# A hybrid decoder block on eight cores: row tiles transposed earlier, five weight places, a spread bias table and residual rows in pieces

## The chip, the cores and the metric

The kernel is one program on the 8 NeuronCores of one Trainium2 chip, four on each die. Cores 2b and 2b+1 share batch row b: each computes 8 of its 16 blocks of 128 tokens and projects keys and values for all 16. Nothing passes between cores. The metric is the device time of the slowest core in microseconds (us).

## The reference, cut to what matters

```python
h = _rmsnorm(x, norm1_g)
q, k, v, q_i, k_i, w_i, u_b, v_b, g_a, g_b = _split_cols(h @ w_in)    # 10320 columns
q, k, k_i = rmsnorm(q), rmsnorm(k), rmsnorm(k_i)                      # per head of 128; k_i: 64
score = sum_h w_i[t, h] * relu(q_i[t, h] . k_i[s]); sel = top_k(score, 256)    # causal
out_a = softmax(q . k[sel] * scale + rel_bias[t5_bucket(t - s)]) @ v[sel]      # 8 heads of 128
out_b = gelu(u_b) * (tril(w_spatial) @ rmsnorm(gelu(v_b)) + b_spatial)
merged = sigmoid(g_a) * (out_a @ w_proj_a) + sigmoid(g_b) * (out_b @ w_proj_b)
x = x + merged @ w_out
x = x + (silu(h2 @ w_ffn_gate) * (h2 @ w_ffn_up)) @ w_ffn_down        # h2 = rmsnorm(x)
```

## The kernel before, in words

Engines get their instructions from Python lists. `Prog` adds the waits: each `Buf` remembers its last writer and its readers, and an engine waits for those semaphores in its own order. A later instruction never overtakes a waiting one, on any engine or DMA queue. A normalized chunk of four tiles has one `Buf` (`B_h[hx]`), so a projection that reads one tile waits for the last tile written into that chunk.

`Dense` is a list of small steps with costs. `unit` adds one output tile as steps of four matmuls, in one of three PSUM banks; `norm_post` sends a Square to ScalarE (ACT) at once and the rest (a matmul with ones at L425, Ln, Exp, and the scaling on VectorE, DVE) one step later. `Stream` holds the weights in order, 256 columns a block: two DMAs of 512 KB as bf16 from the POOL queue, cast on the way. A place is loaded again when its block was last used. Before, the ring has three places.

**The first list, D0**, has these stages. In the v stage, row tiles 0 to 7 are loaded by SP (`x_load`, three buffers), normalized (`x_norm`: Square, Ln, Exp on ACT, one scaling on DVE), transposed on PE (L405, 16 transposes into banks 5 and 6), copied out by ACT and DVE, and projected by v blocks 0 to 3. `prep` puts the norm of tile t+1 ahead of the transposition of tile t. In the k stage, 16 units (4 blocks) alternate with the bias table: `table_item` makes one of 16 tables with two matmuls in one bank (L534), two Exps into one of four buffers `e1`, and a store of 192 KB to `fscr` by SP; tables (0, h) and (1, h) use the same buffer. `xt` transposes tiles 8 to 15 during k and q. Then come two units of the indexer's key (ki), 16 of q, 16 of the indexer's query (qi) and 8 small ones of its weights (wi, 16 columns).

**Attention** (441 to 1141 us in the profile) works through 8 query blocks. A second list, DD, is pulled into it by shares of estimated time: two ki units, the other half of k and v, and the gates g_a and g_b, whose tanh goes to `gscr`.

**The third list, D3**, has the v_b and u_b projections, the spatial gating (`sgu_z`), the projections by w_pa and w_pb in blocks of 8 matmuls per bank, w_out, and the feed-forward part. `gl_load` fetches the gates again (8 DMAs of 256 KB for each c2), and `x1_load` fetches the residual rows (8 tiles of 1 MB). The latter stands 40 steps, five blocks, ahead of the end of w_pa/w_pb for six tiles, and at the end for two.

Of the kernel before, what the change touches and what calls it, by code (L numbers as in the profile page):

```python
# [8 lines left out]
BF16 = mybir.dt.bfloat16  # L9
# [168 lines left out]
def build(ncores=8):  # L178
# [31 lines left out]
    with ExitStack() as es:  # L210
# [66 lines left out]
        RING = [R(3 + 8 * i, 8 * KB, BF16, "p (c n) -> p c n", c=16) for i in range(3)]  # L277
        B_ring = [Buf('ring%d' % i) for i in range(3)]
# [21 lines left out]
        class Stream:  # L300


            def __init__(self):
                self.specs = []
                self.left = {}
                self.got = {}
                self.next = 0
# [4 lines left out]

            def load(self, i):
                slot, b = RING[i % 3], B_ring[i % 3]
# [9 lines left out]
            def pump(self):  # L324
                while self.next < len(self.specs) and (self.next < 3 or self.left.get(self.next - 3) == 0):
                    self.load(self.next)
                    self.next += 1
# [61 lines left out]
        def norm_tile(xb_, xn_, Bxb, Bxn, scol, Bs, Bg):  # L389
            sc = st[:, scol:scol + 3]  # L390
            act(xn_, xb_, AF.Square, (Bxb,), (Bxn, Bs), accum_out=sc[:, 0:1])
            act(sc[:, 1:2], sc[:, 0:1], AF.Ln, (Bs,), (Bs,), scale=1.0 / D, bias=EPS)
            act(sc[:, 2:3], sc[:, 1:2], AF.Exp, (Bs,), (Bs,), scale=-0.5)
            dve('stt', (Bxb, Bs, Bg), (Bxn,), out=xn_, in0=xb_, scalar=sc[:, 2:3], in1=GB, op0=ALU.mult, op1=ALU.mult)
# [20 lines left out]
        norm_banks = {'b': [3, 4], 'n': 0}  # L415
# [27 lines left out]
        def x_load(i):  # L443
            dma_sp(XB[i % 3], x_perm[i * 128:(i + 1) * 128, :], (), (B_xb[i % 3],))
# [14 lines left out]
        x_load(2)  # L459
# [25 lines left out]
        def ki_block():  # L485
            sp = []
            for j in range(2):
                for dup in range(2):
                    sp.append((w_in[j * 1024:(j + 1) * 1024, 4096:4160], 8 * j, 64 * dup))
            return WS.block(sp)  # L490
# [39 lines left out]
        def table_item(q, h):  # L530
            i4 = (q * 8 + h) % 4
            pi = 7
            for u0, u1 in ((0, 512), (512, 768)):
                P.op('pe', lambda e, u0=u0, u1=u1: e.matmul(psb[pi][:, 0:u1 - u0], Lh[:, h, :], oh3[:, q, u0:u1],  # L534
                                                            start=True, stop=True), (B_lh, B_oh), (PS[pi],))
                act(e1[i4][:, u0:u1], psb[pi][:, 0:u1 - u0], AF.Exp, (PS[pi],), (B_e1[i4],))
            base = (q * 8 + h) * 128 * 768
            dma_sp(Fscr[base:base + 128 * 768].rearrange("(r u) -> r u", u=768), e1[i4], (B_e1[i4],), (B_F[q * 8 + h],))
# [48 lines left out]
        def xt():  # L587
# [16 lines left out]
        for hx in (HO0, HT0):  # L604
            ki_unit(D0, kib, hx)
# [7 lines left out]
        B_qTn = [Buf(), Buf()]  # L613
        for b in range(4):
            for cc in range(2):
                for n in range(2):
                    q_unit(qb[b], b, cc, n)
            D0.add(0.5, xt)

# [5 lines left out]
        def wi_unit(tt):  # L625
            n = tt // 4

            def cons(pi):
                dve('copy', (PS[pi],), (B_wt,), out=wtok[:, tt, :], in_=psb[pi][:, 0:16])
            tm_unit(D0, wib, lambda c: hX[n][:, c, (tt % 4) * 128:(tt % 4 + 1) * 128], B_h[n], 16, cons)  # L630
# [4 lines left out]
        for tt in range(8):  # L635
            wi_unit(tt)
# [3 lines left out]
        kib2 = ki_block()  # L640
# [14 lines left out]
        for hx in (HO1, HT1):  # L655
            ki_unit(DD, kib2, hx)
        DD.mark('ki')
# [314 lines left out]
        for k in range(1, 9):  # L972
            if k == 4:
# [447 lines left out]
```

How the kernel before makes its waits and increments, by code:

```python
            def run(name, e):  # L1301
                for waits, fn, inc in P.q[name]:
                    for k, v in waits:
                        e.wait_ge(sems[k], v)
                    if fn is None:
                        continue
                    ins = fn(e)
                    ins.then_inc(sems[inc[0]], inc[1])
```

## Time and profile before

| | |
|---|---|
| three runs | 2462.30, 2698.13, 2724.69 us; median 2698.13 |
| profiled execution | 2464.36 us, span 2462.8 us (core 3; all cores 2431.7 to 2462.8) |
| busy PE, DVE, ACT, POOL | 87%, 33%, 23%, 10% of the span |
| chain that ended last | PE 69%, DVE 13%, DMA 7%, issue 6%, ACT 4% |
| DMA | 222.43 MB moved, mean 90 GB/s |

One execution is shown, on its slowest core. "L262 <- DVE arena L246" reads: the instruction of line 262 waited for a semaphore that the one of line 246 raised. PE is TensorE's matmul. "Busy" at the granted clock 0.5 means 1.2 GHz, at 1.0 it means 2.4 GHz; a mean between them is a mix of the two.

### The profile page before, as it was taken

Reading aid. Unit: us, or ns where it says so; the run is one execution under the profiler, and the core shown is the slowest. Engines: PE = TensorE matmul, PEld = TensorE weight load, DVE = VectorE, ACT = ScalarE, POOL = GpSimd, SP = SyncE. Lnnn points to the kernel's source line nnn. Section 1 sums busy time; section 2 is a strip of 40 time slices with the busy share of each in tenths; the row PEclk is TensorE's granted clock in tenths of the full one; section 3 lists DMA queues with packets and bytes.
Section 4 is the critical chain, followed back from the end, with each engine's and each line's share of the span. In section 5 each row is a group of like instructions: output and inputs, shape, how many; then the busy total and the mean of one; then the engine's idle time right before and its main releaser. Section 6 shows DMA issues by size and latency. Waiting matters only on the chain.

```text
span 2462.8 us, 36680 instructions; the slowest of 8 cores (2431.7 to 2462.8 us)
## 1 busy us (share of the span) xinstructions
PE 2154.8 (87%) x13626; PEld 1247.6 (51%) x13626; DVE 818.3 (33%) x1589; ACT 562.8 (23%) x945; POOL 240.1 (10%) x280
## 2 busy tenths in 40 slices
PE   3656599777898798989989698999999999999999
PEld 2532244323653434347644386444448864444688
DVE  1101131566776867673155324101111110111111
ACT  2314362334344343444300003100000000000000
POOL 0010011000000000000101110111111111111010
PEclk8878799888999999999999899999999999999999
DMA  8274475422333535357649963656546565555485
GB/s 189 69 98 80 76 119 55 65 35 47 48 52 78 112 69 103 65 108 164 78 71 235 220 85 52 79 74 77 77 62 80 77 86 75 77 78 71 63 146 116
DMA packets 319566, 222.43 MB, mean 90 GB/s; under 512 B 25376, under 2 KB 293920, under 8 KB 316064
## 3 DMA queue, kind: packets, MB, share of 16 engines
q0 software_dynamic: 281152, 137.94, 45.1%
q1 hardware_dynamic: 38240, 82.15, 10.1%
q8 instruction: 112, 1.84, 0.3%
q14 instruction: 62, 0.51, 0.1%
HBM read 329.66 MB, written 29.88 MB: 146 GB/s over the span
## 4 chain that ended last, share of the span: by engine, by line
PE 69%; DVE 13%; DMA 7%; issue 6%; ACT 4%; SPq 1%; DVEq 0%; POOL 0%; ACTq 0%; POOLq 0%
PE ps L262 49%; PE ps L1256 12%; DVE arena L244 8%; ACT arena L239 4%; PE ps L740 3%; DVE arena L243 3%; DMA arena<-w_pb 2%; DMA arena<-w_in 2%; PE ps L752 2%; DVE arena L245 2%; DMA fscr<-arena 1%; DMA arena<-w_out 1%; DMA arena<-c_oh 1%; SPq L253 1%; PE ps L405 1%
## 5 line engine op out<-in xcount | busy, mean ns | idle before, releaser
L262 PE MATMUL ps<-arena 128*128 128x512 bf16 (+2 forms) x8384 | 1618.8, 350 | 101.4 <-DVE arena L246 31.0
L262 PEld LDWEIGHTS ps<-arena 128*128 128x128 bf16 x8384 | 816.3, 100 | 796.6 <-issue 142.2
L239 ACT ACTIVATE arena<-ps 128x512 f32<-128x512 f32 (+4 forms) x459 | 264.9, 580 | 1244.0 <-PE ps L262 1066.8
L1256 PE MATMUL ps<-arena 128*128 128x256 bf16 x2816 | 307.7, 273 | 3.0 <-DVE arena L243 3.0
L1256 PEld LDWEIGHTS ps<-arena 128*128 128x128 bf16 x2816 | 275.4, 98 | 35.7 <-issue 3.9
L243 DVE TENSOR_TENSOR arena<-ps,arena 128x512 bf16<-128x512 f32 (+2 forms) x128 | 84.2, 658 | 585.4 <-PE ps L262 540.4
L239 ACT ACTIVATE arena<-ps,arena 128x512 bf16<-128x512 f32 (+1 forms) x312 | 199.7, 647 | 194.5 <-PE ps L752 86.4
L256 POOL DMA_DIRECT2D arena<-w_in x106 | 92.8, 883 | 1117.5 <-PE ps L262 464.0
L245 DVE SCALAR_TENSOR_TENSOR arena<-arena 128x1 f32<-128x1 f32 (+2 forms) x256 | 107.9, 424 | 273.6 <-ACT arena L239 248.4
L244 DVE TENSOR_SCALAR_CACHE_REDUCE arena<-arena 128x512 bf16<-128x512 f32 (+6 forms) x112 | 173.2, 1546 | 14.4 <-DVE arena L245 0.5
L239 ACT ACTIVATE arena<-arena 128x2048 bf16<-128x2048 f32 (+3 forms) x135 | 97.4, 721 | 278.9 <-DVE arena L245 257.6
L243 DVE TENSOR_TENSOR arena<-arena 128x512 bf16<-128x512 bf16 (+9 forms) x297 | 136.3, 469 | 47.4 <-ACT arena L239 16.6
L244 DVE TENSOR_SCALAR arena<-ps,arena 128x512 bf16<-128x512 f32 (+1 forms) x152 | 107.0, 708 | 117.1 <-PE ps L752 105.4
L243 DVE TENSOR_TENSOR arena<-arena,ps 128x256 f32<-128x256 f32 x128 | 53.9, 421 | 255.8 <-PE ps L1256 250.5
L245 DVE SCALAR_TENSOR_TENSOR arena<-ps,arena 128x256 f32<-128x256 f32 (+1 forms) x116 | 66.1, 569 | 198.2 <-ACT arena L239 128.7
L740 PE MATMUL ps<-arena 128*128 128x512 bf16 (+1 forms) x304 | 89.2, 370 | 20.0 <-ACT arena L239 11.3
L887 PE MATMUL ps<-arena 128*128 128x129 bf16 x576 | 59.4, 221 | 50.7 <-DVE arena L243 24.5
L887 PEld LDWEIGHTS ps<-arena 128*128 128x128 bf16 x576 | 37.6, 98 | 66.7 <-issue 65.1
L256 POOL DMA_DIRECT2D arena<-w_down x48 | 41.1, 859 | 301.7 <-PE ps L1256 227.0
L256 POOL DMA_DIRECT2D arena<-w_up x44 | 38.4, 878 | 303.1 <-PE ps L262 290.9
L534 PE MATMUL ps<-arena 128*128 128x512 bf16 (+1 forms) x32 | 11.7, 365 | 61.5 <-ACT arena L239 49.9
L245 DVE SCALAR_TENSOR_TENSOR arena<-arena,ps 128x512 f32<-128x512 f32 x64 | 43.9, 687 | 57.6 <-PE ps L262 33.3
(39 smaller groups left out, 486.4 us busy)
## 6 DMA issues: line engine op xcount, KB each, us to landing
arena<-w_in POOLq DMA_DIRECT2D x96, 512.0 KB, 7.9
arena<-x_perm SPq DMA_DIRECT2D x24, 1024.0 KB, 9.6
arena<-w_gate POOLq DMA_DIRECT2D x44, 512.0 KB, 7.3
arena<-w_up POOLq DMA_DIRECT2D x44, 512.0 KB, 7.1
gscr<-arena SPq DMA_DIRECT2D x64, 256.0 KB, 2.4
arena<-gscr SPq DMA_DIRECT2D x64, 256.0 KB, 9.4
arena<-w_down POOLq DMA_DIRECT2D x32, 512.0 KB, 7.5
arena<-w_out POOLq DMA_DIRECT2D x16, 512.0 KB, 9.7
```

The lines of the kernel that those rows point to most:

```text
L239: return P.op('act', lambda e: e.activation(out=out, in_=in_, func=func, **kw), reads, writes)
L243: 'tt': lambda e: e.tensor_tensor(**kw),
L244: 'ts': lambda e: e.tensor_scalar(**kw),
L245: 'stt': lambda e: e.scalar_tensor_tensor(**kw),
L253: return P.dma('sp', lambda e: e.dma_start(out=out, in_=in_), reads, writes, append)
L256: return P.dma('pool', lambda e: e.dma_start(out=out, in_=in_), reads, writes, append)
L262: ins = e.matmul(out, pairs[i][0], pairs[i][1], start=(i == 0), stop=(i == n - 1))
L405: ins = e.transpose(pv[:, c * 128:(c + 1) * 128], xn_[:, cc * 128:(cc + 1) * 128], ident)
L740: P.op('pe', lambda e, h=h, rt=rt: e.matmul(psb[G[4]][:, 0:wc], Dg[:, h, :], rt[:, 0:wc], start=(h == 0), stop=(h == 15)), (B_dg, B_rt[(2 ...
L752: P.op('pe', lambda e, a=a, pi=pi: e.matmul(psb[pi][:, 0:wc], qsrc[64 * a:64 * a + 64, p, q0:q0 + 128], kiT2[64 * a:64 * a + 64, c0:c0 + w ...
L887: ins = e.matmul(psb[po][:, hh * 130:hh * 130 + 129], PT[pti][:, (j - g0) * 128:(j - g0 + 1) * 128], V[:, j, h, 0:129], start=(j == 0), st ...
L1256: ins = e.matmul(psb[tt][:, 0:256], aT[:, f0 + c, tt * 128:(tt + 1) * 128], slot[:, c, 0:256], start=(f0 + c == 0), stop=(f0 + c == 21))
```

## The change

In the v stage, tile 1 is transposed ahead of the first projection, and later tiles one to two projections ahead of where they stood; the copies out of PSUM now stand ahead of the next tile's norm on ACT. The ring has five places up to the end of the q blocks (two lie where qi is written later), three after that. Three loads of row tiles (2, 4 and 6) wait until weight blocks 0, 1 and 2 have landed. The table's inputs load at the start; each table is two parts, in banks 4 and 7, one part after every second step of the k stage. All four ki units and the wi units stand between q and qi and use one block of 80 columns, doubled by a DVE copy. The gates' first two loads stand after six v_b units. The residual rows are 32 loads of 256 KB, in four column pieces.

```diff
@@ ring and its places
-        RING = [R(3 + 8 * i, 8 * KB, BF16, "p (c n) -> p c n", c=16) for i in range(3)]
+        RING = [R(o, 8 * KB, BF16, "p (c n) -> p c n", c=16) for o in (3, 11, 19, 111.5, 119.5)]
+            def place(self, i):
+                return i % 5 if i < self.wide else (i - self.wide) % 3
...
-        norm_banks = {'b': [3, 4], 'n': 0}
+        norm_banks = {'b': [3], 'n': 0}
...
@@ v stage
+        GATE = {2: 0, 4: 1, 6: 2}
...
             x_norm(i)
             if i + 3 < 16:
-                x_load(i + 3)
+                x_load(i + 3, (WS.use(GATE[i + 3])[1],) if i + 3 in GATE else ())
 
         WS.pump()
+        x_load(2, (WS.use(GATE[2])[1],))
         xstep(0)
+        xstep(1)
+        table_loads()
+        x_tr(0)
...
-        order = [(0, 0), (1, 0), (2, 0), (0, 1), (1, 1), (2, 1), (3, 0), (3, 1), (4, 0), (4, 1),
-                 (0, 2), (1, 2), (2, 2), (3, 2), (4, 2), (5, 0), (5, 1), (5, 2), (6, 0), (6, 1), (6, 2),
-                 (7, 0), (7, 1), (7, 2)]
...
-                def prep(t=t):
-                    if t + 1 < 8:
-                        xstep(t + 1)
-                    x_tr(t)
-                D0.add(0.5, prep)
+        order = [(0, 0), (1, 0), (2, 0), (3, 0), (0, 1), (1, 1), (2, 1), (3, 1), (4, 0), (4, 1), (5, 0), (5, 1),
+                 (0, 2), (1, 2), (2, 2), (3, 2), (4, 2), (5, 2), (6, 0), (6, 1), (6, 2), (7, 0), (7, 1), (7, 2)]
+        before = {0: 1, 1: 2, 2: 3, 6: 4, 8: 5, 14: 6, 18: 7, 21: 8}
+
+        def x_next(t):
+            x_tr(t)
+            if t + 1 < 16:
+                xstep(t + 1)
+        for n_, (t, b) in enumerate(order):
+            if n_ in before:
+                D0.add(0.5, lambda t=before[n_]: (x_tr(t) if t < 8 else None, xstep(t + 1) if t < 8 else None))
...
@@ k stage
-                D0.add(0.5, lambda b=b, cc=cc: (table_item(0, 2 * b + cc), table_item(1, 2 * b + cc)))
-                if cc == 1:
-                    D0.add(0.5, xt)
+        parts = [(q, h, p) for h in range(8) for q in range(2) for p in range(2)]
+        mixed = []
+        for j, it in enumerate(D0.q[k0:]):
+            mixed.append(it)
+            if j % 2 == 1:
+                q_, h_, p_ = parts[j // 2]
+                mixed.append((0.2, lambda q_=q_, h_=h_, p_=p_: table_part(q_, h_, p_)))
+            if j % 16 == 8:
+                mixed.append((0.5, xt))
...
@@ after q
+        D0.add(0.1, ki_dup)
+        for tt in range(8):
+            wi_unit(tt)
+        for hx in (HO0, HO1, HT0, HT1):
+            ki_unit(D0, kib, hx)
...
-        for hx in (HO1, HT1):
-            ki_unit(DD, kib2, hx)
-        DD.mark('ki')
...
@@ gates and residual rows
-        D3.add(0, late_bufs)
-        D3.add(0, lambda: (gl_load(0), gl_load(1)))
+        D3.q.insert(24, (0, lambda: (late_bufs(), gl_load(0), gl_load(1))))
...
-        D3.add(0, lambda: x1_load(range(6)))
-        D3.q.insert(mark_x1 - 40, D3.q.pop())
-        D3.add(0, lambda: x1_load((6, 7)))
+        D3.add(0, lambda: (x1_bufs(range(6)), x1_load(0, range(6))))
+        D3.q.insert(mark_x1 - 24, D3.q.pop())
+        D3.add(0, lambda: (x1_bufs((6, 7)), x1_load(0, (6, 7)), x1_load(1, range(8))))
...
+            if b in (0, 2):
+                D3.add(0, lambda b=b: x1_load(2 + b // 2, range(8)))
```

Below, the order of instructions at three places, of before and of the changed kernel. First PE from the program's start (128x128 are a tile's transposes, 128x256 are v units of 16 matmuls). Before:

```order
L1310 UNCONDITIONAL_BRANCH
L405 MATMUL ps<-arena 128x128 x16
L262 MATMUL ps<-arena 128x256 x16
L405 MATMUL ps<-arena 128x128 x16
L262 MATMUL ps<-arena 128x256 x16
L405 MATMUL ps<-arena 128x128 x16
L262 MATMUL ps<-arena 128x256 x64
```

The change:

```order
L1342 UNCONDITIONAL_BRANCH
L416 MATMUL ps<-arena 128x128 x32
L262 MATMUL ps<-arena 128x256 x16
L416 MATMUL ps<-arena 128x128 x16
L262 MATMUL ps<-arena 128x256 x16
L416 MATMUL ps<-arena 128x128 x16
L262 MATMUL ps<-arena 128x256 x64
L416 MATMUL ps<-arena 128x128 x16
L262 MATMUL ps<-arena 128x256 x32
```

Two tiles are transposed ahead of the first unit instead of one, and later tiles moved up as well. Second, PE in the k stage, one pair of units (128x512 x16 in all per unit; L534, now L542, is the table, L425, now L436, the matmul with ones). Before:

```order
L262 MATMUL ps<-arena 128x512 x4
L425 MATMUL ps<-arena 128x512
L262 MATMUL ps<-arena 128x512 x16
L425 MATMUL ps<-arena 128x512
L262 MATMUL ps<-arena 128x512 x12
L534 MATMUL ps<-arena 128x512
L534 MATMUL ps<-arena 128x256
L534 MATMUL ps<-arena 128x512
L534 MATMUL ps<-arena 128x256
L405 MATMUL ps<-arena 128x128 x16
```

The change, with a tile's transposition in it:

```order
L436 MATMUL ps<-arena 128x512
L416 MATMUL ps<-arena 128x128 x16
L262 MATMUL ps<-arena 128x512 x4
L542 MATMUL ps<-arena 128x512
L262 MATMUL ps<-arena 128x512 x8
L542 MATMUL ps<-arena 128x256
L262 MATMUL ps<-arena 128x512 x4
L436 MATMUL ps<-arena 128x512
L262 MATMUL ps<-arena 128x512 x4
L542 MATMUL ps<-arena 128x512
L262 MATMUL ps<-arena 128x512 x8
L542 MATMUL ps<-arena 128x256
```

Four table matmuls that stood in a row now have eight matmuls of a unit between any two. Third, SP in D3 (one piece of the difference):

```order
-L253 DMA arena<-gscr 128x512 x56
-L253 DMA arena<-x_perm 128x2048 x6
-L253 DMA arena<-gscr 128x512 x8
-L253 DMA arena<-x_perm 128x2048 x2
+L253 DMA arena<-gscr 128x512 x64
+L253 DMA arena<-x_perm 128x512 x16
 L253 DMA arena<-c_g2b 128x2048
+L253 DMA arena<-x_perm 128x512 x16
```

All loads of gates now stand ahead of the residual rows, and these are a quarter as wide.

## Rows read from the trace of the kernel before

**Rows 1.** The page's second part: granted TensorE clock in 40 slices, in tenths
```profile
PEclk8878799888999999999999899999999999999999
```

**Rows 2.** Windows of PE: us, length, busy (instructions), granted clock, DMA share, GB/s
```profile
0.00:158.40 158.40, 84.18 (x644) 0.84 0.60 120
158.40:309.60 151.20, 89.74 (x371) 0.78 0.45 83
309.60:441.20 131.60, 129.49 (x752) 1.00 0.58 81
441.20:1141.00 699.80, 581.76 (x3743) 0.96 0.41 72
1275.50:1416.50 141.00, 115.94 (x588) 0.93 0.99 211
1416.50:1490.00 73.50, 73.50 (x662) 0.98 0.65 83
1545.00:1844.00 299.00, 297.59 (x1384) 1.00 0.56 72
```

**Rows 3.** Waits of PE, 0 to 158 us: us in total, times, longest
```profile
PE ps L262 <- DVE arena L246: 31.0, 6, 5.7
PE ps L262 <- DMA arena<-w_in: 24.0, 2, 12.8
```

**Rows 4.** Waits of PE, 158 to 310 us
```profile
PE ps L534 <- ACT arena L239: 49.9, 24, 7.9
PE ps L534 <- DMA arena<-c_oh: 11.5, 1, 11.5
```

**Rows 5.** Timeline of PE, 0 to 130 us: start, duration, operation, idle before
```profile
31.95 3.57 PE L262 MATMUL ps<-arena 128*128 128x256 bf16 x16 [12.75 <-DMA arena<-w_in]
...
41.73 3.57 PE L262 MATMUL ps<-arena 128*128 128x256 bf16 x16 [4.61 <-DVE arena L246]
...
124.77 5.40 PE L262 MATMUL ps<-arena 128*128 128x256 bf16 x48 [1.86 <-DVE arena L243]
```

**Rows 6.** DMA view, 10 to 32 us: queue, packets, MB, share
```profile
q1 hardware_dynamic: 729, 4.19, 56.1%
q0 software_dynamic: 2601, 1.31, 53.3%
```

**Rows 7.** DMA view, 32 to 60 us
```profile
q0 software_dynamic: 3678, 1.85, 58.1%
```

**Rows 8.** Tile view of w_in, 0 to 60 us: the first six weight DMAs
```profile
DMA to landing us min/median/max: 26.9/33.9/43.9
```

**Rows 9.** Timeline of all engines around the transposition of tile 6
```profile
108.07 1.06 PE L405 MATMUL ps<-arena 128*128 128x128 bf16 x16
...
108.66 1.90 ACT L239 ACTIVATE arena<-arena 128x2048 bf16<-128x2048 f32 x1
...
111.18 1.02 ACT L239 ACTIVATE arena<-ps 128x1024 bf16<-128x1024 bf16 x1
...
113.62 0.68 DVE L246 COPY arena<-ps 128x1024 bf16<-128x1024 bf16 x1
```

**Rows 10.** Tile view of fscr, 0 to 345 us: stores and skewed copies
```profile
  ACT arena L239: 34.3, 8
...
DMA to landing us min/median/max: 1.9/3.5/7.6
```

**Rows 11.** Tile view of c_oh
```profile
DMA to landing us min/median/max: 16.4/16.4/16.4
```

**Rows 12.** Timeline of PE in the q projection
```profile
350.06 3.62 PE L262 MATMUL ps<-arena 128*128 128x512 bf16 x16
```

**Rows 13.** Waits of PE, 1141 to 1560 us
```profile
PE ps L262 <- DMA arena<-w_pb: 18.7, 2, 17.0
...
PE ps L262 <- DMA arena<-w_out: 2.7, 1, 2.7
```

**Rows 14.** Timeline of SP, 1000 to 1560 us
```profile
1343.44 4.00 SPq L253 DMA_DIRECT2D arena<-x_perm  x6
```

More of the change, by code:

```diff
@@ L306, in __init__ @@
                 self.got = {}
+                self.last = {}
+                self.wide = 0
                 self.next = 0
@@ L311, in block, with free @@
                 return len(self.specs) - 1
+            def place(self, i):
+                return i % 5 if i < self.wide else (i - self.wide) % 3
+            def free(self, i):
+                p = self.last.get(self.place(i))
+                return p is None or self.left.get(p) == 0
             def load(self, i):
-                slot, b = RING[i % 3], B_ring[i % 3]
+                self.last[self.place(i)] = i
+                slot, b = RING[self.place(i)], B_ring[self.place(i)]
                 first = True
@@ L324, in pump @@
             def pump(self):
-                while self.next < len(self.specs) and (self.next < 3 or self.left.get(self.next - 3) == 0):
+                while self.next < len(self.specs) and self.free(self.next):
                     self.load(self.next)
@@ L458, in build @@
         dma_sp(csm, c_sm, (), (B_c,), append=True)
-        x_load(2)
         def pos_of(hx, i):
@@ L485, in ki_block @@
         def ki_block():
[L486 to L490, printed above, removed]
+            return WS.block([(w_in[j * 1024:(j + 1) * 1024, 4096:4176], 8 * j, 64) for j in range(2)])
         def ki_unit(dn, blk, hx):
@@ L528, in table_head, with table_part @@
             dve('copy', (B_lh,), (B_lh,), out=Lh, in_=lsel.unsqueeze(2).broadcast_to([128, 8, 128]))
-        def table_item(q, h):
+        def table_part(q, h, part):
             i4 = (q * 8 + h) % 4
[L532 to L538, printed above, removed]
+            pi = (4, 7)[part]
+            u0, u1 = ((0, 512), (512, 768))[part]
+            P.op('pe', lambda e: e.matmul(psb[pi][:, 0:u1 - u0], Lh[:, h, :], oh3[:, q, u0:u1], start=True, stop=True),
+                 (B_lh, B_oh), (PS[pi],))
+            act(e1[i4][:, u0:u1], psb[pi][:, 0:u1 - u0], AF.Exp, (PS[pi],), (B_e1[i4],))
+            if part:
+                base = (q * 8 + h) * 128 * 768
+                dma_sp(Fscr[base:base + 128 * 768].rearrange("(r u) -> r u", u=768), e1[i4], (B_e1[i4],),
+                       (B_F[q * 8 + h],))
         def table_skew(q):
@@ L615, in build, with ki_dup, wi_unit, cons @@
             for cc in range(2):
-                for n in range(2):
-                    q_unit(qb[b], b, cc, n)
+                q_unit(qb[b], b, cc, 0)
             D0.add(0.5, xt)
+            for cc in range(2):
+                q_unit(qb[b], b, cc, 1)
+        def ki_dup():
+            slot, b = WS.use(kib)
+            dve('copy', (b,), (b,), out=slot[:, :, 0:64], in_=slot[:, :, 64:128])
+        def wi_unit(tt):
+            n = tt // 4
+            def cons(pi):
+                dve('copy', (PS[pi],), (B_wt,), out=wtok[:, tt, :], in_=psb[pi][:, 0:16])
+            unit(D0, kib, lambda s_, c: hX[n][:, c, (tt % 4) * 128:(tt % 4 + 1) * 128], lambda s_, c: s_[:, c, 128:144], 16,
+                 lambda pi: psb[pi][:, 0:16], (B_h[n],), cons, 0.12)
+        D0.add(0.1, ki_dup)
[3 more added lines that the diff above has]
+            ki_unit(D0, kib, hx)
         def qi_unit(blk, b, cc, n):
@@ L623, in qi_unit, with qi_place @@
             fm_unit(D0, blk, cc, lambda c: hX[n][:, c, :], B_h[n], cons)
[L625 to L630, printed above, removed]
+        def qi_place():
+            for i in range(2):
+                B_qi[i].absorb(B_ring[3:5])
+        D0.add(0, qi_place)
         for b in range(4):
@@ L1153, in build, with x1_bufs, x1_load @@
         ob = [wblock(w_out, 256 * b, 256) for b in range(8)]
-        def x1_load(ts):
+        B_x1 = [None] * 8
+        def x1_bufs(ts):
             for tt in ts:
-                B_x1[tt] = Buf(after=tuple(B_gv) + tuple(B_vn) if tt < 6 else tuple(B_uT))
-                dma_sp(x1[tt], x_perm[xrow[tt]:xrow[tt] + 128, :], (), (B_x1[tt],))
+                B_x1[tt] = [Buf(after=tuple(B_gv) + tuple(B_vn) if tt < 6 else tuple(B_uT)) for _ in range(4)]
+        def x1_load(c4, ts):
+            for tt in ts:
+                dma_sp(x1[tt][:, 512 * c4:512 * c4 + 512], x_perm[xrow[tt]:xrow[tt] + 128, 512 * c4:512 * c4 + 512], (),
+                       (B_x1[tt][c4],))
         mark_x1 = len(D3.q)
-        D3.add(0, lambda: x1_load(range(6)))
-        D3.q.insert(mark_x1 - 40, D3.q.pop())
-        D3.add(0, lambda: x1_load((6, 7)))
+        D3.add(0, lambda: (x1_bufs(range(6)), x1_load(0, range(6))))
+        D3.q.insert(mark_x1 - 24, D3.q.pop())
+        D3.add(0, lambda: (x1_bufs((6, 7)), x1_load(0, (6, 7)), x1_load(1, range(8))))
         def o_unit(b, tt):
```

45 lines of the change are left out of this document (17 added, 28 removed).

## The prediction

> **What bounds the kernel now.** I read the clock in slices and the windows first. From 1545 us on PE is busy 297.59 of 299 us at a granted clock of 1.00 [rows 1, 2]: nothing of the change is there, and nothing can be won. The holes lie in front. Up to 158.4 us (v stage) PE is busy 84.18 us at clock 0.84; from there to 309.6 us (k stage) 89.74 of 151.20 us at 0.78; then up to 441.2 us (ki, q, qi, wi) it is full, 129.49 of 131.60 us at 1.00. A second hole is 1275.5 to 1416.5 us (w_pa, w_pb), where DMA is busy 0.99 of the time and PE idles 25 us [rows 2]. The waits name the causes. In the v stage the projection waits six times, 31.0 us, for DVE's copy of the tile just transposed, and twice, 24.0 us, for weights: 12.8 us for the first block and the other 11.2 for the fourth, which has no place before [rows 3]. In the k stage it is 49.9 us of table matmuls behind ACT, and 11.5 us for the one-hot table c_oh [rows 4]. A wait costs more than its length: after 4.61 us of idleness a unit of 16 matmuls took 3.57 us, after 1.86 us three took 5.40, so 1.80 each [rows 5]; the first went at 1.2 GHz, the others at 2.4.
>
> I sum against the profiled execution, 2464.4 us (span 2462.8 and 1.6 around it). The median of the three runs is 9.5% above it, the lowest within 0.1%; my number is to be held against runs like the profiled one. A difference of 2% (49 us) is about what a measurement of this kernel can tell from no change.
>
> **V stage, 158.4 us before.** First weights: before, the hardware queue moved 4.19 MB and the software queue 2601 packets in the 22 us from 10 to 32, both about half of the engines [rows 6]; alone, the latter moved 3678 packets in 0.581 x 28 = 16.3 us, 226 a us against 118 [rows 7]. A block is 2048 packets. Now only tiles 0 and 1 and the gain vector (3 MB) compete, gone by some 15 us, since tile 2 waits for the block. About 700 packets are then done, the rest takes 6 us: block 0 lands at 21 to 25 us instead of 32. The first unit must also wait for tile 1's transposition, because the chunk has one `Buf`; that ends at about 25, so it hides. Then the gate costs: tile 2 is asked for at 24, its 1 MB takes 5 us at the rate of [rows 6], the norm 5.0 (the Square starts at 108.66, the DVE copy behind the scaling at 113.62), transposition and copies 1.9 + 1.0 + 0.7 and latencies [rows 9]: the second unit starts at 40, as before (41.73, [rows 5]). The third follows 9 us later, since tile 3's Square stands behind tile 2's copy. From 49 us on every tile is early: 30 units x 1.80 = 54, four transpositions x 1.06 = 4, two places where the `Buf` still makes a unit wait for the copies just issued (tiles 5 and 7, 3 us each, since the copy no longer stands behind a 1.90 us Square) = 6, one unit at half clock 2. End at 115: **gain 43**. The fourth v block has a place, so its wait is gone; what is late next is the first k block, in the fifth place. The table's inputs take 16.4 us to land [rows 11], hidden by 60 us of v work. Bounds: if the tiles stay 8 us late once more, 33; if block 0 at 21 us carries tile 2 forward, 50.
>
> **K stage, 151.2 us before.** Work of PE: 16 units x 3.62 [rows 12] = 58, with 16 matmuls with ones, 32 table matmuls and four transpositions (1.06 each) 72. ACT has about 15 us of work for 17 us of PE in each block of four units, so it decides after each `xt`: a tile's copy (1.02) and Square (1.90, [rows 9]) and the norm's small steps stand ahead of the unit's Square, and PE waits some 2 us at the next matmul with ones. Then SP: the load of tile i+4 waits for DVE's scaling, and the store of table (0, h) stands behind it. The Exp of (1, h), in the same e1 buffer, waits for that store. Before, ACT waited for stores 8 times, 34.3 us, and stores and copies landed in 1.9 to 7.6 us, median 3.5 [rows 10]; behind a 1 MB load I take 6, of which 4.5 reach PE. Elsewhere a store has a unit's time to land and costs nothing: with a landing of 7.6 the Exp comes less than 2 us late. So 4 x (2 + 4.5) = 26, and 98 in all: **gain 53**. Bounds: 78 when stores land in 1.9 us, 115 when each block loses 10 us to waits and half clock: gain 73 or 36. c_oh is waited for no more.
>
> **Q to wi, 131.6 us before.** Two ki units more, 2 x 3.8 = 7.7. The doubling copy on DVE and the wi units stand behind the last q units' scaling: 3 us for PE where before they ended the list. One bank for the matmul with ones instead of two: the next one waits for an Ln that is long done at a unit's distance of 3.8 us, 0. **Loss 11**, between 8 and 14.
>
> **Attention, 699.8 us before.** 2 x 3.8 us of ki leave the second list; PE is busy 83% [rows 2], and the rest are waits that filler doesn't cure. Between 0 and 8; I take half, **gain 4**.
>
> **W_pa, w_pb and w_out.** SP issued six tiles of 1 MB at 1343 us [rows 14], and PE waited 17.0 us for w_pb, 18.7 in all, and 2.7 for w_out [rows 13], with DMA at 0.99. Now 4 MB of gates load 100 us earlier, under v_b, and 1.5 MB instead of 6 come before the end of w_pb. At the stretch's 211 GB/s (and that is made of 256 KB loads mostly) 8.5 MB less are 40 us of DMA. The 6.5 MB that follow the end run beside w_out, where DMA has 35% of 73.5 us free [rows 2]. The 25 us of idleness nearly vanish, the rest of the stage stays near what DMA can do, 5 left, clock 2 back: **gain 22**, between 8 and 27. The small pieces speak against it. The Trainium skill (DMA: Bandwidth & Descriptors, Anatomy of one DMA and Bandwidth) gives each DMA about 2.0 us fixed and asks for 1 MiB or more for 75% of peak. By it six pieces would take 16 us where [rows 2] give 7, and the sum would be 2362.
>
> **Sum:** 43 + 53 - 11 + 4 + 22 = 111; 2464.4 - 111 = **2353 us**.
>
> **The rivals.**
> - *The row tiles bound the v stage.* With ten weight DMAs in the queue (before six, landing after 26.9 to 43.9 us [rows 8]), tiles 2 to 5 get half of the engines until 70 us. If each of four tiles comes 6 us late, the gain is 19: 2377. For it: DMA share 0.60 over the stage with its first 50 us full. Against: rows 6 give a tile 5 us even then. 10%.
> - *The stall at w_pb turns into one for w_out.* DMA was at 0.99, two more residual pieces follow at the end, and PE's 17 us come back there: gain 5, 2370. Against: 8.5 MB less in the stretch. 12%.
> - *Each small piece costs a time of its own.* SP took 4.00 us for six issues, 0.67 each [rows 14]; the 16 pieces up to the end of w_pb make 11, and if w_out waits that long behind them the sum is 2364. Against: 211 GB/s in a stretch of 256 KB loads. The fixed cost of the page DMA: Bandwidth & Descriptors in the Trainium skill would do the same. 3%.
> - *The k stage fills.* The stores land in 1.9 us, gain 73, and v reaches 50: 2326. 6%.
> - *The spread tables make ACT wait for every store.* The place is the Exp of (1, h), 16 times, a unit after the store of (0, h), now with loads of tiles and of weights in flight. Without waits the stage is 72 us; all else gains 58. Up to 8.6 us of PE's waiting per table (151.2 + 58 - 72 = 137, over 16) the kernel is not slower, and by 2% slower from 11.7. The nearest landings are 7.6 [rows 10] and 16.4 (c_oh beside weights, [rows 11]). At 16.4 each it is 72 + 262 = 334: 2589. At 6 each it is 168: 2423, within 2%. Against: only loads at block ends collide, 4 times in 16. 3% slower, 5% within 2%.
> - *The change doesn't do what it says:* with one `Buf` a chunk, the earlier transposition would only move the wait. The order shows it for units 1 to 3, and I have counted it; if it holds for all eight tiles at 5 us, v gains 25 (weights and clock only): 2371. 4%.
>
> **How the numbers follow.** Forecast 57%, rivals 10, 12, 3, 6, 3 + 5 and 4. The terms' ends together give 2464 - (33 + 36 - 14 + 0 + 8) = 2401 and 2464 - (50 + 73 - 8 + 8 + 27) = 2314; all ends at once are unlikely, and the cases at 2370 to 2377 lie inside, so 2320 to 2392 holds 8 in 10. Faster by over 2% is below 2415: 0.92; within 2% 0.05; slower 0.03.
>
> **What would show it.** First unit near 25 us, second near 40, no wait for the fourth v block, k stage from about 115 to 213, clock 1.00 in nearly all slices from the third on, PE's waits for stores at most four of 5 us; ki in one place, D0 ending near 356; no wait over 5 us for w_pb. Wrong would be: PE waits at the table matmuls or the matmul with ones over 60 us, or a granted clock under 0.9 in the k stage, or a new wait for w_out over 10 us.

## The result

| | before | changed |
|---|---|---|
| runs of the comparison, median | 2580.22 us (2457.32 to 2724.69, 4 runs) | 2381.36 us (2375.76 to 2487.6, 4 runs) |
| profiled execution | 2464.36 us, span 2462.8, core 3 | 2385.37 us, span 2383.8, core 6 |
| ratio of undisturbed runs | | 0.9673 [0.9619, 0.9728] |

The runs of before lie in two groups, near 2460 and near 2700 us; every ratio, and every difference in time below, compares undisturbed runs, while a "measured" time is the median of all. Applied to the profiled 2464.4 us, 0.9673 gives 2383.8. So the change wins 3.3%, some 80 us, where 111 us were forecast. The spans differ by 79.0 us, and that is the number divided up below.

First PE by windows, whose columns are those of [rows 2], on the changed kernel's core 6. The cuts are the first matmul of the k stage, the start of the matmuls behind the stage's last matmul with ones, the first matmul of attention and its end; then w_pa with w_pb, and w_out up to the first transposition of norm 2; and last a stretch of the feed-forward part.

```profile
0.00:115.30 115.30, 73.92 (x641) 0.90 0.93 185
115.30:222.40 107.10, 78.13 (x375) 0.90 0.70 122
222.40:366.90 144.50, 139.90 (x785) 0.98 0.43 64
366.90:1057.30 690.40, 572.82 (x3703) 0.97 0.40 70
1191.90:1305.40 113.50, 101.97 (x459) 0.97 0.97 186
1305.40:1418.10 112.70, 96.10 (x849) 0.94 0.80 141
1545.00:1844.00 299.00, 297.70 (x1739) 1.00 0.58 74
```

Two cuts of [rows 2] don't lie at these events: the first k matmul of before started at 157.7 us, not 158.4, and its 1416.5 lies behind the first block of w_out. At the same events the kernel before has these windows:

```profile
0.00:157.70 157.70, 83.48 (x641) 0.84 0.61 121
157.70:309.60 151.90, 90.44 (x375) 0.78 0.45 83
1275.50:1399.60 124.10, 101.73 (x459) 0.92 0.97 206
1399.60:1498.90 99.30, 94.29 (x849) 0.98 0.76 114
```

So the v stage went from 157.7 to 115.3 us, the k stage from 151.9 to 107.1, the rest of the first list from 131.6 to 144.6, and attention from 699.8 to 690.4. W_pa and w_pb went from 124.1 to 113.5, and w_out from 99.3 to 112.7: together 223.3 before and 226.1 now. The window of the feed-forward part, untouched, is as full as before. The granted clock in slices, against [rows 1]:

```profile
PEclk8989999889999999999999999999999999999999
```

The waits of PE: the first fence is 0 to 117 us, against [rows 3]; the second 117 to 223 us, against [rows 4]; the third 1192 to 1420 us, against [rows 13].

```profile
PE ps L416 <- DMA arena<-c_sm: 17.5, 1, 17.5
PE ps L416 <- DVE arena L245: 16.0, 4, 11.1
PE ps L262 <- DVE arena L246: 7.8, 5, 1.8
```

```profile
PE ps L436 <- ACT arena L239: 28.9, 9, 5.4
```

```profile
PE ps L262 <- DMA arena<-w_out: 14.2, 3, 11.6
PE ps L262 <- DMA arena<-w_pb: 7.4, 2, 5.9
PE ps L262 <- DMA arena<-w_pa: 3.2, 1, 3.2
```

The waits for weights in the v stage (24.0 us) and for the tables (61.4 us) are gone. In their place stand 16.0 us for the norms of row tiles and 28.9 us at the matmul with ones. The wait for w_pb has shrunk, and w_out has one of 11.6 us that was not there.

One core isn't the kernel. Stage lengths as the mean over all eight cores of each profiled execution, in us, cut at the events named above ("q to wi" is the rest of the first list, ki included):

| kernel | v | k | q to wi | attention | w_pa, w_pb | w_out | ratio to before |
|---|---|---|---|---|---|---|---|
| before | 153.7 | 144.4 | 131.7 | 698.0 | 121.1 | 95.6 | 1 |
| changed | 114.6 | 106.8 | 144.9 | 689.9 | 108.2 | 104.6 | 0.9673 |
| v_no_gate | 115.3 | 108.1 | 145.3 | 688.1 | 110.2 | 103.8 | 0.9675 |
| three_places | 126.2 | 105.0 | 145.1 | 690.3 | 109.4 | 105.2 | 0.9708 |
| table_together | 114.2 | 122.1 | 144.2 | 689.7 | 107.0 | 103.7 | 0.9740 |
| e1_own_buffer | 115.0 | 74.6 | 143.0 | 690.3 | 109.7 | 105.6 | 0.9532 |
| before_e1 | 155.2 | 111.7 | 131.5 | 698.9 | 123.3 | 95.3 | 0.9881 |
| ki_back | 114.2 | 108.0 | 137.6 | 697.7 | 110.0 | 105.8 | 0.9684 |
| gates_late | 115.0 | 109.1 | 145.3 | 688.5 | 109.1 | 104.7 | 0.9689 |
| x1_whole | 114.8 | 108.1 | 145.6 | 688.6 | 124.8 | 96.7 | 0.9708 |
| x1_gated | 115.0 | 109.0 | 145.3 | 688.7 | 110.2 | 95.2 | 0.9643 |
| combo | 114.5 | 74.6 | 143.2 | 691.1 | 111.0 | 95.2 | 0.9488 |

By mean w_pa and w_pb won 12.9 us and w_out lost 9.0. The cores of one execution differ by 11 us in the two together before (211.8 to 223.3) and by 25 in the changed kernel (201.3 to 226.1). So one run's slowest core is no measure there; means and ratios are.

### The profile page after: what moved, and what is told of

It reads as the page before. It is cut to its first block, busy times and chain, and to the rows that moved or that the text cites. A ratio compares the mean times of both kernels' runs of the same rounds, so it can differ in the third digit from the quotient of the medians.

```text
span 2383.8 us, 36654 instructions; the slowest of 8 cores (2353.4 to 2383.8 us)
## 1 busy us (share of the span) xinstructions
PE 2136.9 (90%) x13626; PEld 1238.3 (52%) x13626; DVE 820.1 (34%) x1590; ACT 560.3 (24%) x945; POOL 233.5 (10%) x272
## 4 chain that ended last, share of the span: by engine, by line
PE 70%; DVE 14%; DMA 6%; issue 5%; ACT 4%; DVEq 0%; ACTq 0%; POOL 0%; SPq 0%; POOLq 0%
PE ps L262 50%; PE ps L1287 13%; DVE arena L244 8%; ACT arena L239 4%; PE ps L768 3%; DVE arena L243 3%; DVE arena L245 2%; DMA arena<-w_out 2%; PE ps L780 2%; DMA arena<-w_pb 2%; DMA fscr<-arena 1%; DMA arena<-w_in 1%; PE ps L436 1%; PE ps L915 0%; DVEq L1336 0%
## 5 line engine op out<-in xcount | busy, mean ns | idle before, releaser
L262 PEld LDWEIGHTS ps<-arena 128*128 128x128 bf16 x8384 | 811.7, 99 | 745.3 <-issue 95.6
L256 POOL DMA_DIRECT2D arena<-w_in x98 | 86.1, 889 | 1040.6 <-PE ps L262 434.0
L239 ACT ACTIVATE arena<-arena 128x2048 bf16<-128x2048 f32 (+4 forms) x135 | 97.4, 721 | 288.7 <-DVE arena L245 263.5
L915 PE MATMUL ps<-arena 128*128 128x129 bf16 x576 | 58.7, 220 | 51.7 <-DVE arena L245 23.6
L768 PE MATMUL ps<-arena 128*128 128x512 bf16 (+1 forms) x304 | 89.2, 373 | 17.6 <-ACT arena L239 10.3
L416 PE MATMUL ps<-arena 128*128 128x128 bf16 x384 | 29.7, 234 | 47.0 <-DVE arena L245 26.2
L256 POOL DMA_DIRECT2D arena<-w_gate x44 | 38.4, 878 | 233.4 <-PE ps L262 225.5
```

The source lines that it names most:

```text
L239: return P.op('act', lambda e: e.activation(out=out, in_=in_, func=func, **kw), reads, writes)
L256: return P.dma('pool', lambda e: e.dma_start(out=out, in_=in_), reads, writes, append)
L262: ins = e.matmul(out, pairs[i][0], pairs[i][1], start=(i == 0), stop=(i == n - 1))
L416: ins = e.transpose(pv[:, c * 128:(c + 1) * 128], xn_[:, cc * 128:(cc + 1) * 128], ident)
L768: P.op('pe', lambda e, h=h, rt=rt: e.matmul(psb[G[4]][:, 0:wc], Dg[:, h, :], rt[:, 0:wc], start=(h == 0), stop=(h == 15)), (B_dg, B_rt[(2 ...
L915: ins = e.matmul(psb[po][:, hh * 130:hh * 130 + 129], PT[pti][:, (j - g0) * 128:(j - g0 + 1) * 128], V[:, j, h, 0:129], start=(j == 0), st ...
```

## The experiments

Every kernel but before_e1 is the changed one with the edit shown.

### The residual rows

**x1_gated** ties each later group of pieces to a block of w_out that has landed.

```diff
-        def x1_load(c4, ts):
+        def x1_load(c4, ts, blk=None):
+            behind = () if blk is None else (WS.use(ob[blk])[1],)
...
-                dma_sp(x1[tt][:, 512 * c4:512 * c4 + 512], x_perm[xrow[tt]:xrow[tt] + 128, 512 * c4:512 * c4 + 512], (),
-                       (B_x1[tt][c4],))
+                dma_sp(x1[tt][:, 512 * c4:512 * c4 + 512], x_perm[xrow[tt]:xrow[tt] + 128, 512 * c4:512 * c4 + 512],
+                       behind, (B_x1[tt][c4],))
...
-        D3.add(0, lambda: (x1_bufs((6, 7)), x1_load(0, (6, 7)), x1_load(1, range(8))))
+        D3.add(0, lambda: (x1_bufs((6, 7)), x1_load(0, (6, 7))))
...
-            dma_sp(GB, c_g2b, (), (N4['gb'],))
...
-            if b in (0, 2):
-                D3.add(0, lambda b=b: x1_load(2 + b // 2, range(8)))
+            if b in (0, 1, 2):
+                D3.add(0, lambda b=b: x1_load(b + 1, range(8), b + 1))
+            if b == 3:
+                D3.add(0, lambda: dma_sp(GB, c_g2b, (WS.use(ob[4])[1],), (N4['gb'],)))
```

> The changed kernel, but the residual pieces really wait for their place: piece 1 of all tiles is loaded behind the landing of w_out block 1, piece 2 behind block 2, piece 3 behind block 3, the gain vector behind block 4. In the changed kernel nothing held SP back, so 6.5 MB of pieces and 1 MB of gains were queued within 58 us beside the w_out blocks, and PE waited 11.6 us for the third of them. Theory 1 (the burst delays the w_out blocks): the wait of 11.6 us is under 2, w_out takes 100 to 103 us instead of 112.7, ratio to before 0.963, 10 us below the changed kernel. Theory 2 (the 2 KB rows make the transfers dearer, or DMA lacks capacity over the whole stretch): the wait only moves, w_out stays at 110 to 114 us, ratio as the changed kernel, 0.967.

Measured: 2372.05 us, ratio 0.9643 [0.963, 0.9656]. To see why, look first at SP in the changed kernel: start, duration, operation.

```profile
1279.42 37.06 SPq L253 DMA_DIRECT2D arena<-x_perm  x16
1316.64 0.39 SPq L253 DMA_DIRECT2D arena<-c_g2b  x1
1317.12 20.10 SPq L253 DMA_DIRECT2D arena<-x_perm  x16
```

All 32 pieces and the 1 MB of c_g2b are in the queue within 58 us. The last pieces stand after w_out's third block in the program, but nothing on SP waits for that block, so SP passes them on at once. PE at that time:

```profile
1307.57 15.80 PE L262 MATMUL ps<-arena 128*128 128x256 bf16 x128 [2.15 <-DMA arena<-w_out]
1323.82 14.13 PE L262 MATMUL ps<-arena 128*128 128x256 bf16 x128 [0.45 <-DMA arena<-w_out]
1349.56 66.14 PE L262 MATMUL ps<-arena 128*128 128x256 bf16 x592 [11.61 <-DMA arena<-w_out]
```

The DMA view of 1305.4 to 1418.1 us has the burst in its two lines by slices (40 of 2.8 us), and the landings below them:

```profile
DMA  9999999999999999973100991009910199101990
GB/s 178 115 208 193 291 232 320 285 232 282 282 228 200 204 259 245 195 97 49 21 9 6 145 198 23 6 11 145 198 18 6 16 150 196 19 0 11 183 173 5
...
arena<-x_perm SPq DMA_DIRECT2D x26, 256.0 KB, 17.2
arena<-w_out POOLq DMA_DIRECT2D x12, 512.0 KB, 14.7
```

The engines are full for 48 us, while PE waits for w_out, and more than half idle for the 65 that follow, when nobody needs them. With the gate, PE and SP of x1_gated (its slowest core) show:

```profile
1297.38 108.12 PE L262 MATMUL ps<-arena 128*128 128x512 bf16 x911 [5.23 <-DMA arena<-w_pa]
```

```profile
1279.23 72.70 SPq L253 DMA_DIRECT2D arena<-x_perm  x32
```

From 1297 us on PE doesn't stop, through the end of w_pb and all of w_out. W_out takes 95.2 to 95.4 us on each of the eight cores, where the changed kernel has 100.7 to 110.6; by mean that is 9.4 us less, of which w_pa and w_pb take 2.0 back. The time is 7 us shorter than the changed kernel's and 10 shorter than that of its repeat (gates_late, below). That the burst delayed w_out is shown.

**x1_whole** asks what the pieces are worth: tiles of 1 MB again, where before had them.

```diff
...
+                dma_sp(x1[tt], x_perm[xrow[tt]:xrow[tt] + 128, :], (), (B_x1[tt][0],))
...
-        D3.add(0, lambda: (x1_bufs(range(6)), x1_load(0, range(6))))
-        D3.q.insert(mark_x1 - 24, D3.q.pop())
+        D3.add(0, lambda: x1_bufs(range(6)))
+        D3.q.insert(mark_x1 - 40, D3.q.pop())
...
```

> The changed kernel, but the residual rows as before: whole tiles of 1 MB, six of them 40 steps ahead of the end of w_pb, two at the end; all other parts of the change stay. Theory 1: the stall returns to w_pb (a wait of 10 to 17 us) and leaves w_out (no wait over 4 us); w_pa to w_out together take 218 to 226 us, so the time is within 5 us of the changed kernel: the pieces gave nothing. Theory 2 (pieces are dear): the two stages together are 8 us or more shorter than with pieces (226.2), ratio 0.963. If the forecast had been right on the pieces it would be 15 to 20 us slower than the changed kernel, ratio 0.974.

Measured: 2390.67 us, 0.9708 [0.9695, 0.9722], between the two theories and the forecast. PE on its slowest core:

```profile
1298.17 36.92 PE L262 MATMUL ps<-arena 128*128 128x512 bf16 x222 [12.21 <-DMA arena<-w_pb]
1339.83 70.38 PE L262 MATMUL ps<-arena 128*128 128x256 bf16 x628 [4.74 <-DMA arena<-w_out]
```

The wait for w_pb is back, as in [rows 13]. By mean the pieces, with their later place, take 16.6 us off w_pa and w_pb (124.8 to 108.2) and add 7.9 to w_out (96.7 to 104.6); the time is 6 to 9 us shorter with them. Tied to the landings they keep nearly all of the first and lose none of the second. This run doesn't tell what is owed to the size of the pieces and what to their place.

**gates_late** takes the gates' first loads back to their old place in the list.

```diff
-        D3.q.insert(24, (0, lambda: (late_bufs(), gl_load(0), gl_load(1))))
+        D3.add(0, late_bufs)
+        D3.add(0, lambda: (gl_load(0), gl_load(1)))
```

> The changed kernel, but the two first loads of gates stand in the list where they stood before, after the u_b units. The order of instructions on SP is then the same as in the changed kernel, since nothing else stands between the two places on SP and none of the 16 loads waits for PE. Theory: the same time, ratio 0.966 to 0.969, the first 16 loads issued some 3 us after the last attention matmul in both, so this run is also a repeat of the changed kernel. If the place in the list did set the time, they would be issued 100 us later and w_pa would wait 5 to 15 us more, ratio 0.972.

Measured: 2382.73 us, 0.9689 [0.9676, 0.9703], the changed kernel's time. The reason stands on SP: the first row is of before, the second of the changed kernel.

```profile
1143.97 12.83 SPq L253 DMA_DIRECT2D arena<-gscr  x16
```

```profile
1060.41 13.79 SPq L253 DMA_DIRECT2D arena<-gscr  x16
```

Both start 3 us after the end of attention. In before, too, SP had nothing to wait for, and the 4 MB were under way 130 us before the projections began. The order of SP's instructions is the same with and without the edit, so this run serves as a repeat of the changed kernel. It shows how far stages vary: means within 2.3 us.

### The k stage

**e1_own_buffer** gives tables (0, h) and (1, h) different buffers.

```diff
-            i4 = (q * 8 + h) % 4
+            i4 = (2 * h + q) % 4
```

> The changed kernel, but tables (0, h) and (1, h) use different e1 buffers (index (2h + q) mod 4 instead of (8q + h) mod 4), so an Exp waits for the store of two tables before, not of the last one. Theory (the waits of 4.4 to 5.4 us at the matmul with ones, once a block, come from the store that stands behind a row tile's load on SP): PE's waits for ACT in the k stage fall from 29 us to under 14, the stage from 100 to 82 to 88 us, the time by 12 to 18 us, ratio 0.961. Rival (ACT's own work behind the tile's norm makes them): the waits stay above 24 us and the ratio is that of the changed kernel.

Measured: 2345.32 us, 0.9532 [0.9519, 0.9545]. That is 35 us less than the changed kernel, about twice the 12 to 18 expected. The wait at issue, as the changed kernel has it (all engines, around 165 us):

```profile
162.07 0.34 SPq L253 DMA_DIRECT2D arena<-x_perm  x1
162.52 13.98 SPq L253 DMA_DIRECT2D fscr<-arena  x3
...
168.00 1.36 ACT L239 ACTIVATE arena<-ps 128x512 bf16<-128x512 f32 x3 [5.50 <-DMA fscr<-arena]
...
169.23 0.58 PE L436 MATMUL ps<-arena 128*128 128x512 bf16 x1 [4.43 <-ACT arena L239]
...
171.75 3.39 PE L262 MATMUL ps<-arena 128*128 128x512 bf16 x8
...
177.27 1.89 PE L262 MATMUL ps<-arena 128*128 128x512 bf16 x8
```

A row tile's load goes ahead of the store, the Exp into the same buffer waits 5.50 us for that store, PE stops for 4.43 us at the next matmul with ones, and then 8 matmuls take 3.39 us, where 8 take 1.89 a few us later: 1.2 GHz and 2.4. The stage has five such waits, 4.4 to 5.4 us each. With the edit the waits of PE from 117 to 190 us are, and the k stage as a window is:

```profile
PE ps L436 <- ACT arena L239: 5.4, 4, 1.4
```

```profile
114.75:189.43 74.68, 69.30 (x375) 1.00 0.94 156
```

The stage falls from 107.1 us at clock 0.90 to 74.7 at 1.00. Of the 32.4 us, 23.5 are waits (28.9 against 5.4) and 8.8 half clock behind them (PE busy 78.1 against 69.3 for the same matmuls), some 2 us for each of the five. ACT waited for `fscr` six times, 30.2 us, and now never, though stores and skewed copies land no faster (median 3.9 us against 2.2).

**before_e1** is the same edit in the kernel before.

> The kernel before with one index changed: tables (0, h) and (1, h) use different e1 buffers. In its trace ACT waited 34.3 us for stores, 8 times, and PE behind it. Theory (the shared buffer is the costly part of the table already in the kernel before): the k stage falls by 34 us and some clock, 30 to 42 us in all, ratio 0.983 to 0.988. Rival (the four table matmuls in one bank cost the time anyway): less than 12 us, ratio over 0.995.

Measured: 2430.38 us, 0.9881 [0.9867, 0.9895]. PE's waits, 158 to 290 us, against [rows 4]:

```profile
PE ps L534 <- ACT arena L239: 21.1, 24, 1.1
```

29 of the 49.9 us at the tables were the shared buffer, and by mean, with the clock, 32.7 us of stage. What [rows 4] show as table matmuls behind ACT was for the larger part this buffer.

The four kernels together show that the two gains of the k stage are independent. The index is worth 32.7 us without the rebuilding (144.4 to 111.7) and 32.2 with it (106.8 to 74.6); the rebuilding is worth 37.6 with the shared buffer and 37.1 without.

**table_together** keeps all else and puts the four parts of a pair of tables back in a row.

```diff
-            if j % 2 == 1:
-                q_, h_, p_ = parts[j // 2]
-                mixed.append((0.2, lambda q_=q_, h_=h_, p_=p_: table_part(q_, h_, p_)))
+            if j % 8 == 7:
+                for q_, h_, p_ in parts[j // 8 * 4:j // 8 * 4 + 4]:
+                    mixed.append((0.2, lambda q_=q_, h_=h_, p_=p_: table_part(q_, h_, p_)))
```

> The changed kernel, but the four table parts of a head stand together after every second k unit, as before, still in banks 4 and 7 and with the one-hot table loaded early. Theory (spreading gave the gain that was forecast, 30 to 35 us of the k stage's 51, the early one-hot table the rest): the k stage takes 130 to 138 us instead of 100, ratio 0.981. Rival (the waits for the store stay what they are wherever the parts stand): the stage stays within 10 us of 100, ratio at most 0.972.

Measured: 2395.39 us, 0.974 [0.9719, 0.9761], between both expectations. PE's waits, 114 to 243 us:

```profile
PE ps L436 <- ACT arena L239: 32.9, 7, 7.9
PE ps L542 <- ACT arena L239: 7.9, 8, 1.0
```

Spreading alone is worth 15.3 us of stage by mean (122.1 to 106.8). The waits are fewer and longer; that the Exp of (1, h) follows (0, h)'s store at once fits this and was not tested by itself. The other 22 us that the k stage won include the wait for the one-hot table (11.5 us on the slowest core of before, [rows 4]); the two banks and the ACT order are left for the rest, and I didn't separate these.

### The v stage and the filler

**v_no_gate** lets the row tiles load freely.

```diff
-        GATE = {2: 0, 4: 1, 6: 2}
+        GATE = {}
...
-        x_load(2, (WS.use(GATE[2])[1],))
+        x_load(2)
```

> The changed kernel, but the loads of row tiles 2, 4 and 6 do not wait for weight blocks 0, 1 and 2. If the gate costs (PE waits 11.1 us for tile 2 after the first unit): the first unit starts near 32 us instead of 24, the second follows at once near 36 instead of 42, and the v stage ends 0 to 5 us earlier than 117 us. If the gate gives what it was forecast to give: the v stage ends later, at 119 to 124 us. Either is under 0.3% of the time, so the profile decides, not the ratio (0.966 to 0.969).

Measured: 2383.49 us, 0.9675 [0.966, 0.9689]. PE's first units, of the changed kernel and then without gates:

```profile
24.36 3.57 PE L262 MATMUL ps<-arena 128*128 128x256 bf16 x16 [1.47 <-DVE arena L246]
39.01 1.87 PE L416 MATMUL ps<-arena 128*128 128x128 bf16 x16 [11.08 <-DVE arena L245]
42.14 3.32 PE L262 MATMUL ps<-arena 128*128 128x256 bf16 x16 [1.26 <-DVE arena L246]
```

```profile
37.01 3.57 PE L262 MATMUL ps<-arena 128*128 128x256 bf16 x16 [14.15 <-DMA arena<-w_in]
...
43.54 1.91 PE L262 MATMUL ps<-arena 128*128 128x256 bf16 x16 [1.67 <-DVE arena L246]
```

The gate moves the first unit 13 us ahead and pays it back at the second: 42.1 against 43.5. Neither expectation came true: without the gate both units came later than foreseen (37.0 and 43.5, not 32 and 36), and the stage ends at 115.3 us by mean against 114.6. Those 0.7 us are no more than kernels with the same v stage differ (114.2 to 115.0), so the gate's worth can't be told from nothing.

**three_places** leaves the ring three places.

```diff
-        WS.wide = len(WS.specs)
+        WS.wide = 0
```

> The changed kernel with three weight places instead of five from the start. Forecast: the fourth v block waits again for DMA (11 us and 2 of clock), so the v stage ends at 128 to 131 us instead of 117; the first k block then comes later too, but is hidden under the last v block. Ratio 0.972. If the early transposition was what paid and the places were not needed, the stage ends by 122 us, ratio 0.969.

Measured: 2391.21 us, 0.9708 [0.9688, 0.9728]. PE on its slowest core:

```profile
90.32 10.64 PE L262 MATMUL ps<-arena 128*128 128x256 bf16 x96 [1.78 <-DVE arena L246]
111.00 18.42 PE L262 MATMUL ps<-arena 128*128 128x256 bf16 x136 [10.04 <-DMA arena<-w_in]
```

The wait for the fourth block is the 10.04; v is 11.6 us longer, and the k stage 1.8 shorter. The places are worth the wait that they remove, nothing more.

**ki_back** moves two ki units into attention's list again: a block of its own ahead of the second half of k, only HO0 and HT0 in D0.

```diff
-        for hx in (HO0, HO1, HT0, HT1):
+        for hx in (HO0, HT0):
             ki_unit(D0, kib, hx)
...
+        for hx in (HO1, HT1):
+            ki_unit(DD, kib2, hx)
+        DD.mark('ki')
...
```

> The changed kernel, but the two ki units of the second half of the tokens stand in the attention's filler list again, with their own weight block of four small DMAs. Forecast: 7.7 us less before attention, 4 (0 to 8) more in it, so 4 us faster than the changed kernel, ratio 0.9655. If PE is what bounds attention at those places: the same time, ratio 0.967; the trace shows attention at 699 instead of 690 us.

Measured: 2383.23 us, 0.9684 [0.9664, 0.9704]. The stretch from q to wi is 7.3 us shorter (137.6 against 144.9), attention 7.8 longer (697.7 against 689.9): the same work, moved at full price.

### Both edits

**combo** is e1_own_buffer and x1_gated together.

> The changed kernel with both mended parts: tables (0, h) and (1, h) in different e1 buffers, and the residual pieces and the gain vector held back behind w_out blocks 1 to 4. If the two causes are separate, their gains add: 36 us before attention (k stage and its waits) and 10 to 12 between w_pa and w_out, so about 2334 us, ratio 0.949. If the w_out stall is set by DMA capacity over a longer stretch and not by the order of the loads, the second gain is smaller here, ratio 0.953.

Measured: 2335.19 us (2333.20 to 2336.35), 0.9488 [0.9469, 0.9507], 44 us under the changed kernel and the fastest of all. Its k stage:

```profile
114.77:189.24 74.47, 68.71 (x365) 1.00 0.93 155
```

Both gains are there: 74.6 us for the k stage and 95.2 for w_out in the table of stages.

## Why the prediction was right and where it was wrong

The direction was right and the size was not: 111 us forecast, 79.0 us between the profiled executions. The forecast was made for the slowest cores; the last column has the mean over all cores.

| term | forecast | slowest cores | mean |
|---|---|---|---|
| v stage | +43 | +42.4 | +39.1 |
| k stage | +53 | +44.8 | +37.6 |
| q, wi and ki | -11 | -13.0 | -13.2 |
| attention | +4 | +9.4 | +8.1 |
| w_pa, w_pb, w_out | +22 | -2.8 | +3.9 |
| the rest | 0 | -1.8 | +1.3 |

Two terms failed: w_pa, w_pb and w_out, by 25 us, and the k stage, by 8. Attention gave 5 back.

**V stage: right, step by step.** First unit at 24.4 us (25 said), second at 42.1 (40), the third at 49.1, first k matmul at 115.3 (115). PE waits 7.8 us in five places for the DVE copy instead of 31.0 in six, and 16.0 us for norms, as the gate's price foretold. three_places confirms the 11 us of the fourth block. The gate was rightly costed at next to nothing. No run takes back the earlier transposition alone, so its share is read from the waits and not shown by itself. One landing was far off: c_oh, issued at 10.91 us behind ten weight loads, took 70.2 us and not the 16.4 of [rows 11]. It came at 81 us, longer than the 60 us of cover that the prediction named, but 36 us ahead of the first table matmul: that it cost nothing was partly luck.

**K stage: the waits right, the half clock left out.** 107.1 us against 98. The 98 were 72 of work and 26 of waits. The waits came to 28.9: five for a store, 23.6 us together, where four were forecast, and four short ones. Four of the five stores stood behind SP's load of a row tile, as described; the first did not. The other 6 us are work: PE was busy for 78.1 us where the sum had 72, and e1_own_buffer does the same matmuls in 69.3. So the half clock behind the waits, 8.8 us, was put at nothing in the sum, though the prediction says of the v stage that a wait costs more than its length. The mechanism was priced and not followed to its end, either: that the wait exists only because of an index was seen ("in the same e1 buffer"), and before_e1 shows that it had cost the kernel before 33 us already.

**Q to wi: right.** 13.0 us lost, between 8 and 14 foreseen. Window 222.4 to 366.9 us of the changed kernel, and then 309.6 to 441.2 us of before, grouped by form:

```profile
L262 PE MATMUL ps<-arena 128*128 128x512 bf16 x572 | 130.3, 385 | 0.0
```

```profile
L262 PE MATMUL ps<-arena 128*128 128x512 bf16 x540 | 120.5, 379 | 0.0
```

The work on these matmuls grew by 9.8 us, of which 7.7 are the two ki units as said. The rest is half clock behind the k stage's last store wait, which stands just ahead of this window. PE waited 2.5 us for DVE's copies here, where 3 were foreseen.

```profile
222.16 0.38 PE L436 MATMUL ps<-arena 128*128 128x512 bf16 x1 [4.88 <-ACT arena L239]
222.37 5.30 PE L262 MATMUL ps<-arena 128*128 128x512 bf16 x16
```

**Attention: the reason failed.** I took half of 7.6 us since fillers don't cure waits. It gave 9.4, by mean 8.1, and ki_back took it back at 8. A PE busy 83% [rows 2] had no free room for these units.

**W_pa, w_pb and w_out: this step failed**, for 25 of the 32 us missing. W_pa and w_pb gave 10.6 of the 22 (12.9 by mean), and w_out took 13.4 (9.0 by mean). Three things in it were wrong.
- "4 MB of gates load 100 us earlier": they were early before. The order of the list had moved; the queue hadn't. They were 4 of the 8.5 MB less.
- "The 6.5 MB that follow the end run beside w_out": they ran in one burst ahead of w_out's third block, since the queue had nothing to wait for. 14.2 us of waits for w_out ate what w_pb gave. The prediction had named "a new wait for w_out over 10 us" as a sign of being wrong, and had this as a rival, the stall that turns into one for w_out, at 12%. Its price, 5 instead of 22, is nearly the mean of 3.9.
- 22 us was nearly all that the stage had. I read its length on the slowest core of before, 223.3 us; the mean was 216.8, and the shortest of any core in any run, in x1_gated, is 197.6. A stage without a burst gave 11.4 by mean. I also cut the window at 1416.5 us as the end of w_pb, which lay at 1399.6, with the first block of w_out behind it, so some of the 8.5 MB were in the wrong place.

That the small pieces cost a time of their own is not borne out: SP issued 32 of them in 58 us without anyone waiting for SP, and x1_gated, all in pieces, is faster than x1_whole. (The stretch that the prediction called "made of 256 KB loads mostly" held 44 of them, 11.5 of its 29.8 MB, so it was a weak witness.) They may cost a little more of the engines: over 1230 to 1410 us the hardware queue took 27.7% of 16 engines for 16.19 MB in x1_whole, 49 us of an engine per MB, and 32.8% for 16.68 MB in x1_gated, 57; but these two runs differ in the time of the loads as well. By the fixed 2.0 us a DMA in the Trainium skill (DMA: Bandwidth & Descriptors, Anatomy of one DMA) 32 pieces would take 64 us one after another, an estimate; the page fitted it on the software queue, while these pieces go by the hardware queue. Here they overlap, so the rule doesn't decide. The advice to issue a DMA early and wait for it late in the Trainium skill (DMA: Bandwidth & Descriptors, Rules for kernel authors) holds for the table's input c_oh, which no matmul waited for here; against it stands the residual rows' burst, where early issue cost PE 11.6 us.

What stays open: why cores of one execution differ by 11 to 16 us in w_pa and w_pb even where w_out is the same on all (combo, x1_gated); how the k stage's gain splits between the banks, c_oh and ACT's order; and how that of the pieces splits between their size and their place.

## What to carry to other kernels

A place in the program is no time for a queue that waits for nothing: see in its own rows when it issues, and tie a load to the landing of what must not be late, rather than to a line further down. When two producers in a row share a buffer that a DMA still reads, rotate the buffer by the producers' order first; here one index was worth 1.2% before the change and 1.5% after it, nearly what the whole rebuilding of the k stage gave (32 against 38 us by mean). Add the half clock behind a wait to the price of the wait. Price a stage on all cores and against the best core seen, and check where its last instruction lies before cutting the window.

## What the runs showed of the chip

- A wait of 4.4 us of PE cost some 2 us more at half clock: the 8 matmuls behind it took 3.39 us at 1.2 GHz, and 1.89 at 2.4.
- The same load on the software queue landed after very different times: c_oh took 70.2 us right behind ten weight loads at the program's start, and 16.4 in the kernel before [rows 11], right behind two.
- A burst on SP's queue delays loads on POOL's: w_out's 512 KB loads landed in 16.0 us (median) and 42.6 at most in the changed kernel, in 13.1 and 24.5 in x1_gated (slowest cores).
- The cores of one execution differ where PE waits for DMA (w_out 100.7 to 110.6 us in the changed kernel) and hardly where it doesn't (w_out 95.2 to 95.4 in x1_gated).
